# A two-layer hybrid encoder on one core: one chunk handled tile by tile, one piece moved from GpSimd to VectorE, and filler products of 128 columns in place of 512

## The reference, cut to what matters

```
x <- LayerNorm(alpha * x + Mixer(x))            # ph 0 (layer 0), ph 2 (layer 1)
x <- LayerNorm(alpha * x + ChannelMixer(x))     # ph 1 (layer 0), the end (layer 1)
Mixer: one input projection -> gated linear recurrence and windowed attention -> one output projection
ChannelMixer, layer 0: silu(x @ wg) * (x @ wu) @ wd, hidden width 2816
ChannelMixer, layer 1: the same per expert, top 2 of 8 experts for each token
```

## Time and profile before

| | us |
|---|---|
| median of 3 runs | 1039.72 (1039.71 to 1039.80) |
| the profiled execution, whole | 1039.66 |
| its span in the trace | 1037.8 |
| PE busy | 1017.1 |
| DVE busy | 641.6 |
| ACT busy | 534.0 |
| POOL busy | 89.9 |

### The profile page before, as it was taken

How to read it: one execution, slowest core, us unless ns; L and a number is a source line. 1 busy time by engine, 2 the same in 40 slices (tenths; PEclk the granted TensorE clock), 3 DMA queues, 4 the chain that set the end, 5 groups by cost and what they waited for, 6 DMA issues and landing times.

```text
span 1037.8 us, 15344 instructions
## 1 busy us (share of the span) xinstructions
PE 1017.1 (98%) x6042; PEld 777.0 (75%) x6042; DVE 641.6 (62%) x868; ACT 534.0 (51%) x813; POOL 89.9 (9%) x95
## 2 busy tenths in 40 slices
PE   8999999999999999999999999999999999999995
PEld 8987788888899888875667786558777566878552
DVE  6897645545678889971149883119985107988103
ACT  5785443434469677761147772128775116767102
POOL 0004000000200069910000000000000000000000
PEclk9999999999999999999999999999999999999998
DMA  9944545545583669989999999999999999999981
GB/s 370 372 175 165 198 171 198 183 182 203 214 334 134 226 227 371 371 340 397 422 420 421 422 420 418 420 422 422 419 422 416 422 421 421 422 419 422 420 368 43
DMA packets 48155, 343.25 MB, mean 331 GB/s; under 512 B 5377, under 2 KB 5505, under 8 KB 6865
## 3 DMA queue, kind: packets, MB, share of 16 engines
q1 hardware_dynamic: 46656, 336.09, 80.3%
q0 software_dynamic: 992, 5.56, 1.5%
q10 hardware_dynamic: 432, 0.59, 0.2%
HBM read 341.17 MB, written 1.05 MB: 330 GB/s over the span
## 4 chain that ended last, share of the span: by engine, by line
PE 94%; DVE 3%; ACT 1%; DMA 1%; issue 0%; POOL 0%; POOLq 0%; SPq 0%
PE bank L939 15%; PE bank L622 14%; PE bank L624 14%; PE bank L623 13%; PE bank L930 7%; PE bank L796 7%; PE bank L799 7%; PE bank L802 7%; PE bank L892 2%; PE bank L817 1%; PE bank L1022 1%; DVE low L1438 1%; PE bank L899 1%; DVE low L1753 1%; DMA x<-x_d 1%; PE bank L663 1%
## 5 line engine op out<-in xcount | busy, mean ns | idle before, releaser
L1753 DVE TENSOR_TENSOR low<-raw,whi 128x1024 fp32r<-128x1024 f32 x236 | 278.9, 1235 | 29.7 <-ACT whi L1311 29.3
L624 PE MATMUL bank<-whi,al 128*128 128x512 f32 (+1 forms) x624 | 233.5, 374 | 0.0
L1311 ACT ACTIVATE whi<-raw 128x1024 fp32r<-128x1024 f32 x236 | 232.5, 1051 | 0.0
L1438 DVE TENSOR_TENSOR low<-raw,whi 128x1024 fp32r<-128x1024 f32 x108 | 130.8, 1242 | 25.8 <-ACT whi L1119 24.8
L939 PE MATMUL bank<-raw,xg 128*64 128x256 f32 x1264 | 145.2, 380 | 0.0
L622 PE MATMUL bank<-whi,xgh 128*128 128x512 f32 x352 | 142.4, 405 | 0.0
L1804 DVE TENSOR_TENSOR he<-he,bank 128x128 f32<-128x128 f32 x44 | 12.7, 288 | 205.2 <-ACT he L1369 205.2
L624 PEld LDWEIGHTS bank<-whi,al 128*128 128x128 f32 x624 | 117.5, 188 | 22.0
L1119 ACT ACTIVATE whi<-raw 128x1024 fp32r<-128x1024 f32 x114 | 115.9, 1057 | 27.7 <-PE bank L624 17.4
L623 PE MATMUL bank<-low,xgh 128*128 128x512 f32 x328 | 127.9, 390 | 0.0
L939 PEld LDWEIGHTS bank<-raw,xg 128*64 128x64 f32 x1264 | 88.5, 137 | 41.4 <-issue 1.4
(11 more groups left out here) (304 smaller groups left out, 1341.8 us busy)
## 6 DMA issues: line engine op xcount, KB each, us to landing
raw<-W SPq DMA_DIRECT2D x290, 1024.0 KB, 12.7
spare<-W SPq DMA_DIRECT2D x14, 1024.0 KB, 14.4
xT<-W SPq DMA_DIRECT2D x14, 1024.0 KB, 14.9
scr<-gb_d POOLq DMA_DIRECT2D x3, 1024.0 KB, 7.5
x<-x_d SPq DMA_DIRECT2D x2, 512.0 KB, 5.5
raw<-W SPq DMA_DIRECT2D x2, 512.0 KB, 5.9
scr<-wbd_d POOLq DMA_DIRECT2D x2, 512.0 KB, 8.9
spare<-gb_d POOLq DMA_DIRECT2D x1, 1024.0 KB, 10.8
```

What stands on the lines that cost most here:

```text
L624: return nc.tensor.matmul(out, sl, mh, start=False, stop=last, skip_group_check=True)
L1311: nc.scalar.activation(whi[:, q % SPLIT, h * HW:(h + 1) * HW], piece_slot(home(J, i)[0])[:, h * HW:(h + 1) * HW], ACT.Copy).then_inc(hi_rd ...
L1438: V.tensor_tensor(low_of(p)[:, h * HW:(h + 1) * HW], piece_slot(place(p)[0])[:, h * HW:(h + 1) * HW], whi[:, p % SPLIT, h * HW:(h + 1) * H ...
L1753: V.tensor_tensor(low_slot(s)[:, h * HW:(h + 1) * HW], piece_slot(s)[:, h * HW:(h + 1) * HW], whi[:, q % SPLIT, h * HW:(h + 1) * HW].bitca ...
```

## The change

It makes five edits.

1. Each filler product becomes three of 128 columns, which alternate between two stationary blocks. The two fillers before the second mixer go.
2. POOL no longer makes the low part of piece 11. DVE does, one half before `sums(0)` of ph 0 and one half between `scale(0)` and `split_x(1, 0)`.
3. In ph 1, DVE does `split_x(2, 0)` before `sums(1)` and not behind it.
4. The last chunk of the dense channel mixer is turned and split by tiles, with semaphores of its own for tile 0, and the silu of tile 0 waits for tile 0 of B alone (`gu0_ps`). Both output steps of tile 0 then run before the two half steps of tile 1 of chunk 9.
5. In the second mixer the transposes of tile 1 stand after 4 and after 6 of the 8 column blocks of piece 45. Before, they stood after 6 and after 8 (`ks`; one block is three products).

```diff
-WARM = {"start": 8, "x1": 7, "mixer": 0, "dense": 2, "last_mixer": 0, "tile": 4, "tile2": 2, "split": 3, "rank": 7,
+WARM = {"start": 8, "x1": 7, "mixer": 0, "dense": 0, "last_mixer": 0, "tile": 4, "tile2": 2, "split": 3, "rank": 7,
...
-POOL_PIECES = (MIXP, MIXP + 1, MIXP + FFP + 1)
+POOL_PIECES = (MIXP + 1, MIXP + FFP + 1)
...
-                for _ in range(n):
-                    nc.tensor.matmul(bank[:, b, :], src[:, 0:P], src, start=True, stop=True)
+                for i in range(3 * n):
+                    nc.tensor.matmul(bank[:, b, 0:P], src[:, i % 2 * P:(i % 2 + 1) * P], src[:, 0:P], start=True,
+                                     stop=True)
...
+                        if i == STEP[("B", NCH - 1)] and t == 0 and k == 3:
+                            last.then_inc(gu0_ps, 1)
...
+                def turn_last(t):
+                    pe.wait_ge(h_rdy, NT * (NCH - 1) + t + 1)
+                    for k in range(2):
+                        last = nc.tensor.transpose(bank[:, 6 + t, k * P:(k + 1) * P], hs[:, t, k * P:(k + 1) * P],
+                                                   ident[:])
+                    last.then_inc(hT_ps if t else hT0_ps, 1)
+
                 p = MIXP + T_MID
                 pe.wait_ge(hTl_rdy, NCH - 1)
+                turn_last(0)
                 half(p, 0, NCH - 2, 0)
-                turn_h(NCH - 1)
+                turn_last(1)
                 half(p, 1, NCH - 2, 0)
+                pe.wait_ge(hTl0_rdy, 1)
+                down(p + 1, part(NCH - 1), False, True, 0)
                 half(p, 0, NCH - 2, 1)
+                half(p, 1, NCH - 2, 1)
                 pe.wait_ge(hTl_rdy, NCH)
-                down(p + 1, part(NCH - 1), False, True, 0)
-                half(p, 1, NCH - 2, 1)
                 down(p + 1, part(NCH - 1), False, True, 1)
...
                 if ph == 0:
-                    split_x(1, 0)
+                    lo_half(last_piece, 1)
+                if ph < 2:
+                    split_x(ph + 1, 0)
                 sums(1)
-                if ph == 1:
-                    split_x(2, 0)
...
+                if l == 0:
+                    lo_half(p0 + MIXP, 0)
                 norm(2 * l, p0 + MIXP)
```

More of the change, by code:

```diff
@@ L335, in build @@
         res_rdy = sem("res_rdy")
+        hT0_ps = sem("hT_ps_last_chunk_tile0")
+        hTh0_rdy = sem("hTh_rdy_last_chunk_tile0")
+        hTl0_rdy = sem("hTl_rdy_last_chunk_tile0")
         eps_rdy = sem("eps_rdy")
@@ L571, in _ @@
                     low(POOL_PIECES[0])
-                    low(POOL_PIECES[1])
                 pool.wait_ge(x_rdy, 2 * NT * (2 * l + 1))
@@ L575, in _ @@
                     pool.dma_start(gb.rearrange("p a n -> p (a n)"), gb_d[1]).then_inc(gb_in, 16)
-                    low(POOL_PIECES[2])
+                    low(POOL_PIECES[1])
                 else:
@@ L680, in mixer @@
                     rows(p0, 2, 0, True)
-                    rows(p0 + 1, 3, 0, ks=range(0, 6))
+                    rows(p0 + 1, 3, 0, ks=range(0, 4))
                     transpose_x(2 * l, 1, (0,))
+                    rows(p0 + 1, 3, 0, ks=range(4, 6))
+                    transpose_x(2 * l, 1, (1,))
                     rows(p0 + 1, 3, 0, ks=range(6, KT))
-                    transpose_x(2 * l, 1, (1,))
                     rows(p0, 2, 1, True)
@@ L1251, in high_h, with high_last @@
                     nc.scalar.activation(hbuf[c % 2][0], bank[:, 6:8, 0:FC], ACT.Copy).then_inc(hTh_rdy, 1)
+                def high_last(t):
+                    if t == 0:
+                        act.wait_ge(hT0_ps, 1)
+                    else:
+                        act.wait_ge(hT_ps, NCH)
+                    nc.scalar.activation(hbuf[(NCH - 1) % 2][0][:, t, :], bank[:, 6 + t, 0:FC],
+                                         ACT.Copy).then_inc(hTh_rdy if t else hTh0_rdy, 1)
                 nc.scalar.activation(junk[:, 4:5], ident[:, 0:1], ACT.Silu)
@@ L1259, in dense @@
                         c = H_AT[i]
-                        act.wait_ge(used, 2 * (MIXP + STEP[("B", c)] + 1))
                         if c:
@@ L1263, in dense @@
                         for t in range(0 if c else 1, NT):
+                            if c == NCH - 1 and t == 0:
+                                act.wait_ge(gu0_ps, 2)
+                            else:
+                                act.wait_ge(used, 2 * (MIXP + STEP[("B", c)] + 1))
                             nc.scalar.activation(hs[:, t, :], bank[:, t, 0:FC], ACT.Silu).then_inc(silu_rdy, 1)
@@ L1271, in dense @@
                                                  scale=ALPHA).then_inc(seed_rdy, 1)
+                    if i == T_MID:
+                        high_last(0)
                     hi_half(MIXP + i + 2, 0)
                     if i == T_MID:
-                        high_h(NCH - 1)
+                        high_last(1)
                     if i == FFP - 1:
@@ L1431, in lo_half @@
             def lo_half(p, h):
[L1432 to L1435, removed]
+                after_pool = h == 0 and p - 1 in POOL_PIECES
+                if after_pool:
                     dve.wait_ge(pool_lo, 2 * POOL_PIECES.index(p - 1) + 2)
@@ L1439, in lo_half @@
                                 whi[:, p % SPLIT, h * HW:(h + 1) * HW].bitcast(F32),
-                                ALU.subtract).then_inc(lo_rdy, 2 * by_pool + 1)
+                                ALU.subtract).then_inc(lo_rdy, 3 if after_pool else 1)
             def lo(p):
@@ L1669, in low_h, with low_last @@
                     V.tensor_tensor(hl, bank[:, 6:8, 0:FC], hh.bitcast(F32), ALU.subtract).then_inc(hTl_rdy, 1)
+                def low_last(t):
+                    if t == 0:
+                        dve.wait_ge(hTh0_rdy, 1)
+                    else:
+                        dve.wait_ge(hTh_rdy, NCH)
+                    hh, hl = hbuf[(NCH - 1) % 2]
+                    V.tensor_tensor(hl[:, t, :], bank[:, 6 + t, 0:FC], hh[:, t, :].bitcast(F32),
+                                    ALU.subtract).then_inc(hTl_rdy if t else hTl0_rdy, 1)
                 for i in range(FFP):
@@ L1680, in dense @@
                         continue
+                    if i == T_MID:
+                        low_last(0)
                     lo_half(MIXP + i + 2, 0)
                     if i == T_MID:
-                        low_h(NCH - 1)
+                        low_last(1)
                     lo_half(MIXP + i + 2, 1)
```

## The result

| | median, us | all executions, us | ratio to before, 95% interval |
|---|---|---|---|
| before | 1039.72 | 1039.58 to 1039.86 (5) | |
| after | 1046.19 | 1045.91 to 1051.81 (5) | 1.0083 (1.0069 to 1.0096) |

The change makes the kernel slower, by 0.6% going by the medians and by 0.8% going by the ratio in the table. The forecast was 1039.7, and the range ended at 1045.5. Two of the five executions of after took 1051.6 and 1051.8. The profiled one is the fastest of the five. It took 1045.91 whole, with a span of 1044.0, so what the trace shows accounts for the fastest execution and not for the long ones.

A forecast was written before the change was run, and what follows sets the result against it. PE was taken to bound the kernel, so the change could act only at four places: +0.2 (start) - 1.6 (first mixer's end) + 0 (seam) + 1.4 (router) = 0.0 against 1039.66, giving 1039.7 us; range 1037.9 to 1045.5.

The forecast's parts named there:

- The small filler: Start and router: one product of 128 columns costs 0.11 us warm, 0.22 at 1.2 GHz.
- Rival 1: All remaining fillers: the narrow product runs at the plain float32 rate, 0.22 us each, 0.43 cold; 1051; chance 0.15.
- rival 2: Start and router: the load hides, pace 0.066 to 0.08, so both cost nothing; 1038.1; chance 0.08.
- The start: First fillers and transposes: input products late by +0.2 us, ends 0 and +0.6, clock rising at about 5.6.
- cold paces beyond 7 us: At the start: a sign that, if seen, would make the prediction wrong.
- rival 3: At the start: the clock rises late, as columns stream only half of the time; +5.5, 1045; chance 0.06.
- The end of the first mixer: PE's wait on DVE's low half goes; -1.6 us, ends -1.8 and +0.5.
- Rival 4: End of the first mixer: POOL takes the turn at 85.6, nothing is won there; 1041.6; chance 0.05.
- The seam: Dense channel mixer to second mixer: new wait for x, paid back at tile 1; 0, ends -0.4 and +0.5.
- The router: 19 fillers become 57, so the gather starts later; +1.4 us, ends +1.0 and +2.0.
- the fifth group: Last group of fillers in the router, before the gather: +0.3 us.
- the fourth group: Router: 21 small fillers at 0.11 us end at 367.85, making their successor +1.1 us late.

The follow-up runs named there:

- experiment 3: The changed kernel with 128-column fillers at the start alone and 512-column fillers in the router; 1042.41 us.
- experiment 1: The changed kernel with every filler one product of 512 columns again, all other edits kept; 1038.11 us.
- experiment 4: The changed kernel with two products of 256 columns for each filler, alternating stationary blocks; 1038.08 us.
- experiment 5: The changed kernel with 512 columns at the start and two products of 128 columns for each filler in the router; 1043.42 us.
- experiment 7: The changed kernel with 512-column fillers at the start and no fillers in the router; 1042.65 us.
- experiment 6: The changed kernel, three products of 128 columns for each filler, but always the same stationary block; 1050.18 us.
- experiment 8: The kernel before with only the low part of piece 11 moved from POOL to DVE, fillers of 512 columns; 1038.69 us.

## Why the prediction was wrong

**The small filler: right.** Forecast 0.11 warm and 0.22 cold, measured 0.114 to 0.118 (the groups in the router before the fall) and 0.216. It was read off the load (0.106 at 8 columns, rows 7). Rival 1 (0.22 warm) and rival 2 (0.066 to 0.08) both fell with that. The Trainium skill (TensorE: Matmul & The Clock Gate, section Back-to-back issue gap), whose 81 ns would have made the sum 1.5 us lower, does not agree with this case: 114 ns is the least that 128 columns took here with these operands.

**The start: +1.43, forecast +0.2 (ends 0 and +0.6).** The step that failed here is "some 19 run until the clock rises at about 5.6". That time was taken over from the trace before, where other products had run. With 128 columns the rise came a little behind 8.2. All 24 fillers and the eight transposes stayed cold, which is 6.61 - 6.25 and another 0.6; in place of 2.3 the 21 took 2.55. The prediction's own sign, cold paces beyond 7 us, came true. This is rival 3 by its kind, which got 0.06. Its price was +5.5. The profiled executions of after and of experiment 3 cost less (1.4 and 1.8), but experiment 3 as a whole stands 1.6 to 5.6 us above experiment 1, at the median 4.3, which is nearer the rival's price than the forecast's.

**The end of the first mixer: right.** -1.6 forecast, with ends -1.8 and +0.5; measured -1.88 here and, by the edit alone, -1.75 in the trace at that place, or -1.88 against its 0.13 later start. The mechanism is the one named: DVE's half at 77.59 shares its time with nobody, and two take 2.35 us where one took 3.41. Rival 4 did not come: DVE's last half there took 1.45 and not 3.4, and it was POOL's second half that stood. That is the turn of the earlier trace rows again, where POOL's second half took 3.36 us and its first, with nobody ahead of it, 2.4:

```profile
79.59 3.36 POOL L467 TENSOR_TENSOR low<-raw,whi 128x1024 fp32r<-128x1024 f32 x1
```


**The seam: right in its steps.** Forecast 0, measured +0.19 here and +0.2 to +0.3 by itself. The square root was due at 277.3 and came at 276.82 in a kernel that was 0.45 ahead; the new wait of 0.8 is 0.70; the wait at tile 1 is gone. The input products were +0.40 late (forecast +0.35), and edit 5 paid back 0.21 of the forecast 0.36.

**The router: +6.3, forecast +1.4 (ends +1.0 and +2.0).** This term broke the forecast. The step that failed is the pace: "21 x 0.11 = 367.85", the fifth group's +0.3 and the gather are all priced at full clock, and a fall of the clock stands at nothing in the sum. Up to the fourth group the working holds. That group starts at 365.31 against 364.98, which is +0.59 with the 0.26 by which the kernel was ahead; the working said +0.55. Then the clock falls. The 21 fillers take 3.01 us where 21 x 0.115 are 2.42, so 0.6 is lost. From 368.32 to the first expert product there are 9.91 us; before there were 5.40 (366.79 to 372.19), and forecast were 5.7. That is another 4.2. Together 4.8 us: some 10 us at half pace lose half of their length, as the 0.50 of the clock row says.

The working had held the clock constant in the router without asking. What came nearest to a reason is said against rival 3, on the start: "in the router 16 products of 8 columns twice did not bring it down". Those groups stood between fillers of 512 columns, which the change takes away. Experiments 1, 4, 5 and 7 show the same groups with fillers of 512 and 256 columns (clock 1.00), of 128 and with none (0.50). The row was evidence on the mixture and was read as evidence on its part. Of a filler the prediction asked only what it costs, and never what it is there for. A rival "the small fillers don't hold the clock in the router", worked out from the rows of before, would have taken the stretch from 364.98 to 372.19 at half pace: up to +7.2 us on top, and 1039.7 to 1046.9.

The Trainium skill (TensorE: Matmul & The Clock Gate, section What's actually happening) says that the clock is set by "how busy the PE has been recently". By the busy share of the trace this case does not agree: 8.00 of 8 us from 358 to 366, and then 0.50.

**The sum.** +0.2 - 1.6 + 0 + 1.4 = 0.0 stands against +1.43 - 1.88 + 0.19 + 6.30 = +6.04. Of this 1.2 and 4.8 are the clock's. Both were counted as what goes beyond the forecast's own working, so that the rest of these two terms fits (0.2 and 1.5) shows little; by the clock alone the router's share is half of some 10 us at 0.50, 5.0, which would leave 1.3. The two terms without the clock are off by -0.28 and +0.19, and that these nearly cancel is luck. Three figures of the prediction don't follow from their own terms: the first fillers' end comes to 1.43 + 19 x 0.22 + 5 x 0.11 = 6.16 and not 6.25; the ends of the four terms add up to -1.2 and +3.6, or 1038.5 to 1043.3, and not to 1038.7 to 1041.5; and rival 4, with nothing won in the first mixer, comes to 1041.3 and not 1041.6. None of them reaches the 1046.2.

**What stays open.** Why two of five executions of after, and two of four in experiment 6, are at 1051.7. Their mean clock (0.990 against 0.991 to 0.992) explains 1 to 2 us of the 5.6, an estimate: 0.001 to 0.002 of 1044 us. As that column doesn't show the cold pace of the start, a still later rise there would fit the rest, but no such execution was profiled. The one execution of 2089 us in experiment 3 had twice the usual time, and nothing in these runs explains it. That with fillers in place it is their width that brings the clock down in the router is shown by experiments 1, 4 and 5; by which measure the chip judges it is not.

## What to carry to other kernels

A filler is judged by what it keeps up, not by what it costs: before narrowing one, or a whole stretch of PE, price that stretch at half the clock as a rival, even where PE stays 100% busy. A stretch that holds its clock says nothing about its parts when the wide products between them go. And when a norm's square root stands behind other work on ACT, move it and its table load ahead before taking PE's cover away: here that was worth 0.9 us.

## What the runs showed of the hardware

- Products of 128 columns with their loads, back to back, cost 0.114 to 0.118 us each and let PE appear 100% busy; yet the granted clock went to 0.50 for 10 to 16 us. Products of 256 columns at 0.129 us held it at 1.00 (experiment 4). An unchanged stationary block gave the same pace as an alternating one.
- At the start the pace rose between about 5.0 and 7 us in nine profiled kernels with fillers of 512 or 256 columns, and between about 8.5 and 9.9 in the three with 128. The clock column said 1.00 throughout.
- Once small products are in a place, the time spreads: 1044.6 to 1047.9 (router alone), 1039.7 to 1043.7 (start alone), 1045.9 to 1051.8 (both), where the version with 512 columns and the repaired seam stays within 0.25 us.
- Output transfers of the same size at the end took 2.9 us to the slowest landing in eleven profiled kernels and 3.7 us in one (experiment 8).
- DVE's and POOL's splits that overlap slow each other: 3.41 us for a half of DVE's that takes 1.2 alone. The Trainium skill (SBUF — State Buffer, section SBUF: two separate sides) says that the port pair of the two is a lock held for a whole instruction. The trace agrees: DVE's half behind POOL's first half stood for 2.2 us, about one half of POOL's (2.4), and POOL's second half behind it took 3.36 and not 2.4.
